# Block results stored from ScalarE's queue, the last round's weights in half-width transfers, and three steps of the dense part in another order

## The chip, the cores and the metric

One core of a Trainium2 chip runs the whole program. The metric is the device time of one execution in microseconds (us); the median of three timed runs stands for the kernel. A profile is one further execution, recorded instruction by instruction.

## The reference, cut to what matters

One sequence of 256 tokens with 1,024 features goes through two layers, all in float32. Layer 0 has a mixer (one input projection, attention of 8 heads beside a gated convolution, an output projection) and a SwiGLU of width 2,816. Layer 1 has a state-space mixer, whose tables are computed from parameters, and a top-2-of-8 expert SwiGLU of width 3,584. Each sub-layer is normed, scaled and shifted by values made from a condition vector `c`, and added back through a gate:

```python
h = _ada_norm(x, norm_mix_g[layer], sh_m, sc_m)
...
probs = jax.nn.softmax(logits, axis=-1)
top_p, top_i = lax.top_k(probs, TOP_K)
...
for e in range(N_EXPERTS):
    out = out + gates[:, e:e + 1] * _swiglu(hf, w_gate[e], w_up[e], w_down[e])
```

## The kernel before

Each engine has its own instruction stream; semaphores join them. SyncE (SP) only issues DMAs. Weights come from DRAM in one order through a ring of buffers.

**Dense part.** A piece of weights is 128 rows of 8 KB (1 MB); the ring has 14 places, and SP loads piece n once TensorE has counted `piece_done` to n - 13. TensorE first multiplies the condition by pieces of `mod_w` (L483), then does the input projection, 12 pieces (L499). Ahead of that, VectorE scales the normed input in eight chunks (L1173), and ScalarE adds the shift to each chunk (`shift(0)`, L925): only then is the input of the projection there. In ScalarE's stream `shift(0)` (L941) stands behind five DMA issues: one that loads the small state-space parameters (L937) and four that fill a scratch tensor (L939). Behind it stand the exponential and the sines (L943 to L946), for which VectorE waits at L1223.

**Layer 0's SwiGLU.** `FF_UNITS` = 11 units. For unit f TensorE does gate (one piece), up (one piece), and down of unit f - 1 (one piece); behind each of the three is a slot numbered 3f, 3f+1, 3f+2 in which steps of the state-space tables may stand (`segment`, L638). `side_plan` (L89) gives each of four batches q its four steps s: slots 5+7q+s, so the batches start in slots 5, 12, 19 and 26. Step 0 transposes `bsm`, which VectorE makes in `block_inputs(q)` (L1368, six operations over 128x1024) behind its product of unit 1, 3, 5 or 8 (L1393, the condition at L1397); TensorE waits for it at L611. ScalarE takes each step's result out of PSUM (L989) and sends whole tables to a scratch tensor: `bt_spilled` behind step 1, `ct_spilled` behind step 2, `kc_spilled` behind step 3 (L993 to L1010). SP loads them back when all four batches have been sent. VectorE also computes part of the `mod` values in the same units (`mod_dots`, L1198), each waiting for a 1 MB piece that ScalarE's stream issues (L1016).

**Experts.** Tokens are gathered into blocks of 32, here 22 blocks. The expert width is cut into 7 rounds of 512. In a round each expert has three pairs of pieces (2 MB each: two for gate and up, one for down), and each of its blocks does `gate_up` (L795, 64 matmuls in the trace), ScalarE's Silu (L1088), VectorE's product and transpose, and `e_down` (L804, 32). `gate_up` of block j+1 stands ahead of `e_down` of block j on TensorE. Nine places hold pairs, so a pair is loaded when the third expert before it is through (`pair_plan`, L131; the loads at L415). 168 pairs in all, 24 in a round.

**Last round.** VectorE adds the round's result to a block, multiplies by the gate row (`scale_block`, L1582) and counts `y_scaled`. The blocks of experts 0 to 6 but the last one, here 19, go to the scratch tensor `y_scr`, from which GpSimd fetches each token's two rows by index (L1771) when all have landed (L1765); the last three blocks go through a matmul instead (L832). A store of a block (L431) is one DMA of 128 KB: 32 rows of `y_scr`, seen as 4 quarters x 32 rows x 256 numbers, so 128 pieces of 1 KB. SP's stream issues the stores: those of expert 0 behind the load of pair 158, expert 1's behind 161, expert 2's behind 164 (`STORED_EARLY` = 3), and the rest behind the last load, 167. Behind them is one more load, the final gain (L451). The fetched rows overwrite the place of pair 159.

Of the kernel before, what the change touches and what calls it, by code (L numbers as in the profile page):

```python
# [22 lines left out]
T = 256  # L23
# [63 lines left out]


def side_plan():  # L89

    uses = {("param", 0): 2, ("param", 1): 2, ("param", 2): 1, ("param", 3): 1}
    at = {}
    for q in range(BATCHES):
        for s in range(4):
            at.setdefault(5 + 7 * q + s, []).append(("param", q, s))
    plan, use = {}, 0
    for n in sorted(at):
        for kind, i, s in at[n]:  # L100
            plan.setdefault(n, []).append((kind, i, s, use))
            use += uses[kind, s]
    return plan
# [46 lines left out]
LAST_E = EXPERTS - 1  # L150
FILLS = -(-MOST * BLK // T)
STORED_EARLY = 3
STORE_FROM = PAIRS - STORED_EARLY * STEP
FREE_AT = Y_PAIR // STEP % EXPERTS
# [18 lines left out]
def trunk_kernel(nc, xt_in, pos_in, cols_in, gain_in, consts_in, ssm_in, c_in, rows_in, dense_in, expert_in, ssm_scr, kc_scr, y_scr, out):  # L173
    ctx = ExitStack()
    with ctx:
# [170 lines left out]
        def pair_slot(n):  # L346
            s = PAIR_PLAN[n][0]
            if s < RING // 2:
                return ring[:, 2 * s * PIECE:(2 * s + 2) * PIECE]
            s = MORE - 1 - (s - RING // 2)  # L350
            return more[:, 2 * s * PIECE:(2 * s + 2) * PIECE]

        def pair_sem(n):
            s = PAIR_PLAN[n][0]
            return ring_full[2 * s] if s < RING // 2 else (more_full0, more_full1)[s - RING // 2]

        def pair_full(n):

            s = PAIR_PLAN[n][0]
            dense_uses = sum(parts(m) for m in range(PRE) if m % RING == 2 * s) if s < RING // 2 else 0  # L360
            return pair_sem(n), 16 * (dense_uses + sum(PAIR_PLAN[m][0] == s for m in range(n + 1)))

# [22 lines left out]
        def _(sp):  # L385
# [28 lines left out]
            def load_pair(n):  # L414
                sp.dma_start(pair_slot(n), expert_in[n]).then_inc(pair_sem(n), 16)  # L415

# [4 lines left out]
            for n in range(RING // 2, RING // 2 + SOON):  # L421
                sp.wait_ge(piece_done, AT_GLU)
                load_pair(n)

            def store_rows(upto, e):

                if e == 0:
                    sp.wait_ge(y_stored, 16 * FILLS)
                with sp.Fori(upto[e - 1] if e else 0, upto[e] if e < LAST_E - 1 else upto[e] - 1) as j:
                    sp.wait_ge(y_scaled, j + 2)  # L430
                    sp.dma_start(y_scr[bass.ds(j * BLK, BLK), :].rearrange("i (q n) -> q i n", q=4),  # L431
                                 acc[:, bass.ds(j * 256, 256)]).then_inc(y_stored, 16)

            sp.wait_ge(items_ready, 1)
            upto = blocks_upto(sp)
            for n in range(RING // 2 + SOON, PAIRS):
                prior = PAIR_PLAN[n][1]
                if prior is None:
                    sp.wait_ge(e_gather, GATHERS)
                else:  # L440
                    step, k = divmod(prior, STEP)
                    rnd, e = divmod(step, EXPERTS)
                    sp.wait_ge(gu_done if k < GU else down_done, upto[e] + upto[-1] * rnd)
                load_pair(n)
                if STORE_FROM - 1 <= n < PAIRS - 1 and n % STEP == GU:
                    store_rows(upto, (n + 1 - STORE_FROM) // STEP)

            for e in range(STORED_EARLY, LAST_E):
                store_rows(upto, e)
            sp.wait_ge(gu_done, upto[FREE_AT] + upto[-1] * (ROUNDS - 1))  # L450
# [444 lines left out]
        def _(act):  # L895
# [38 lines left out]
            act.wait_ge(piece_done, AT["mod", 5] + 1)  # L934
            act.dma_start(posi, pos_in.partition_broadcast(P).rearrange("p o t -> p (o t)")).then_inc(pos_loaded, 16)
            act.wait_ge(piece_done, AT["mod", 7] + 1)
            act.dma_start(ssm_par[:, :], ssm_in).then_inc(ssm_loaded, 16)  # L937
            for q in range(BATCHES):
                act.dma_start(kc_scr[q, P:P + GCH * (LB - 1), :].rearrange("a b -> (a b)").rearrange("(p n m) -> p n m", p=P, n=2),  # L939
                              consts_in[:, C_ID + P:C_ID + P + GCH * (LB - 1)].unsqueeze(1).broadcast_to([P, 2, GCH * (LB - 1)])).then_inc(kc_zeroed, 16)  # L940
            shift(0)  # L941
            act.wait_ge(decay_arg, 1)
# [144 lines left out]
            def silu():  # L1087
                return act.activation(e_act_b, PS[:, 0, 0:SLOT], ACT.Silu)  # L1088
# [5 lines left out]
            for e in range(EXPERTS):  # L1094
# [10 lines left out]
                with act.Fori(upto[e - 1] + 1 if e else 1, upto[e]) as j:  # L1105
                    act.wait_ge(gu_done, j + 1)
                    silu().then_inc(silu_ready, 1)
            for rnd in range(1, ROUNDS):
                with act.Fori(0, upto[-1]) as j:
                    act.wait_ge(gu_done, j + upto[-1] * rnd + 1)  # L1110
                    silu().then_inc(silu_ready, 1)
            act.activation(held, consts[:, C_EPS:C_EPS + 1], ACT.Sqrt)
            for t_ in range(2):
# [13 lines left out]
        def _(dve):  # L1127
# [260 lines left out]
            for f in range(FF_UNITS):  # L1388
# [7 lines left out]
                for q in range(1, BATCHES):  # L1396
                    if (5 + 7 * (q - 1) + 2) // 3 + 1 == f:  # L1397
                        block_inputs(q)
# [228 lines left out]
            dve.nop().then_inc(gt_ready, 1)  # L1627
            dve.nop().then_inc(y_scaled, 1)
            with dve.Fori(1, upto_6) as j:
# [46 lines left out]
        def _(pool):  # L1676
# [84 lines left out]
            for rnd in range(1, ROUNDS):  # L1761
                with pool.Fori(0, upto[-1]) as j:
                    pool.wait_ge(gu_done, j + upto[-1] * rnd)
                    load_block(j).then_inc(hbuf_ready, 1)
            pool.wait_ge(y_stored, upto[LAST_E - 1] * 16 + 16 * (FILLS - 1))  # L1765
            pool.sem_inc(y_all, 1)
# [113 lines left out]
```

## Time and profile before

| | us |
|---|---|
| median of 3 runs | 1461.38 (1456.54 to 1463.14) |
| the profiled execution | 1464.03 |
| its span, first to last instruction | 1462.2 |
| TensorE busy | 1370.1 (94%) |
| VectorE busy | 405.6 |
| ScalarE busy | 150.9 |
| GpSimd busy | 169.1 |

The span is 1.8 us shorter than the profiled execution's own time. TensorE's mean granted clock in it was 0.98. Read a timeline row as start, length, engine, line, operation, output <- inputs, count, and in brackets the idle time of that engine just before, with what ended it. PE is TensorE, DVE VectorE, ACT ScalarE, POOL GpSimd, SP SyncE; a q behind the name means its instruction queue, as in a DMA issue. "PEld" is TensorE's weight load.

### The profile page before, as it was taken

To read this page: it belongs to the slowest core of one execution; us is meant where nothing else is said; L and a number is where in the kernel's file an instruction comes from. 1 tells how busy PE (TensorE), PEld (TensorE's weight loads), DVE (VectorE), ACT (ScalarE), POOL (GpSimd) and SP (SyncE) were. 2 spreads that over 40 slices of the span, in tenths; PEclk is the share of its full clock that TensorE was granted. 3 is DMA by queue.
4 is the path that set the end of the run, shared out by engine and by line. 5 is a ranking of instruction groups with operands and counts; after the bars stand their busy time and mean duration, and the time that the engine had idled before them with its cause. 6 is when DMAs were issued, how large, how long until landed. Compare 5 with 4: busy or idle time off the path is not lost.

```text
span 1462.2 us, 43274 instructions
## 1 busy us (share of the span) xinstructions
PE 1370.1 (94%) x19076; PEld 1046.7 (72%) x19076; DVE 405.6 (28%) x1018; ACT 150.9 (10%) x362; POOL 169.1 (12%) x244
## 2 busy tenths in 40 slices
PE   4999999999998898999999989989989999999984
PEld 3887788888787786766677767757757776766762
DVE  2825251453515616111111111111111111111224
ACT  2202121000003104100000000000000000000001
POOL 0000052351401300000000000000000000000001
PEclk8999999999999999999999999999999999999997
DMA  9947578777467507779999999999999999999984
GB/s 383 422 184 302 232 270 282 273 298 284 171 236 288 203 1 308 326 282 427 426 421 414 427 425 414 427 426 408 427 426 411 418 426 424 417 425 426 407 343 170
DMA packets 52818, 499.93 MB, mean 342 GB/s; under 512 B 6668, under 2 KB 13964, under 8 KB 15372
## 3 DMA queue, kind: packets, MB, share of 16 engines
q1 hardware_dynamic: 45708, 463.36, 77.3%
q10 hardware_dynamic: 6400, 32.39, 5.9%
q8 instruction: 120, 1.97, 0.5%
q0 software_dynamic: 576, 2.10, 0.4%
q14 instruction: 14, 0.11, 0.0%
HBM read 485.38 MB, written 16.58 MB: 343 GB/s over the span
## 4 chain that ended last, share of the span: by engine, by line
PE 74%; DMA 15%; DVE 4%; SPq 3%; issue 1%; ACT 1%; POOL 0%; ACTq 0%; POOLq 0%; DVEq 0%
PE PS L795 29%; PE PS L499 19%; PE PS L804 14%; DMA ring<-in_expert_stream 9%; PE PS L649 4%; SPq L431 2%; DMA arena<-in_mod_rows 2%; DVE arena L1137 2%; DMA arena<-in_expert_stream 2%; DMA ring<-in_dense_stream 2%; PE PS L775 2%; PE PS L483 1%; PE PS L531 1%; PE PS L473 1%; PE PS L703 1%
## 5 line engine op out<-in xcount | busy, mean ns | idle before, releaser
L795 PE MATMUL PS<-ring,arena 128*32 128x256 f32 x8288 | 483.2, 381 | 26.1 <-DMA ring<-in_expert_stream 21.7
L795 PEld LDWEIGHTS PS<-ring,arena 128*32 128x32 f32 x8288 | 313.5, 110 | 164.7 <-DMA ring<-in_expert_stream 19.1
L499 PE MATMUL PS<-arena,ring 128*128 128x256 f32 x1408 | 311.9, 383 | 6.2 <-ACT arena L925 4.6
L499 PEld LDWEIGHTS PS<-arena,ring 128*128 128x128 f32 x1408 | 268.7, 192 | 46.0 <-issue 7.1
L804 PE MATMUL PS<-ring,arena 128*32 128x256 f32 x3456 | 208.6, 379 | 0.0
L1137 DVE TENSOR_TENSOR stat<-stat,PS 128x128 f32<-128x128 f32 x154 | 44.4, 288 | 515.4 <-ACT stat L1088 515.4
L804 PEld LDWEIGHTS PS<-ring,arena 128*32 128x32 f32 x3456 | 130.3, 110 | 56.8 <-issue 0.6
L1750 POOL COPY arena<-arena 128x256 f32 x153 | 61.5, 402 | 791.7 <-PE PS L795 791.7
L1137 DVE TENSOR_TENSOR arena<-arena,PS 128x256 f32 (+1 forms) x142 | 63.3, 446 | 238.6 <-PE PS L804 161.6
L1088 ACT ACTIVATE stat<-PS 128x128 f32<-128x128 f32 x154 | 43.2, 280 | 782.4 <-PE PS L795 782.4
L795 PE MATMUL PS<-arena 128*32 128x256 f32 x1568 | 94.8, 379 | 4.3 <-DMA ring<-in_expert_stream 4.3
L804 PE MATMUL PS<-arena 128*32 128x256 f32 x1472 | 89.0, 379 | 0.8 <-DVE consts L1137 0.8
L795 PEld LDWEIGHTS PS<-arena 128*32 128x32 f32 x1568 | 60.0, 110 | 29.3 <-issue 5.7
L649 PE MATMUL PS<-arena,ring 128*128 128x256 f32 x352 | 78.4, 382 | 0.0
L649 PEld LDWEIGHTS PS<-arena,ring 128*128 128x128 f32 x352 | 67.0, 192 | 9.4 <-DVE arena L1137 0.4
L804 PEld LDWEIGHTS PS<-arena 128*32 128x32 f32 x1472 | 56.8, 110 | 23.6 <-issue 1.1
L1137 DVE TENSOR_TENSOR arena<-arena 128x32 f32<-128x32 f32 (+9 forms) x146 | 64.7, 467 | 12.7 <-ACT arena L899 6.5
L899 ACT ACTIVATE arena<-PS 128x512 f32<-128x512 f32 (+4 forms) x72 | 39.2, 560 | 249.4 <-PE PS L499 63.4
L1203 DVE SCALAR_TENSOR_TENSOR arena<-arena 128x1024 f32<-128x1024 f32 x28 | 41.2, 1509 | 78.2 <-DMA arena<-in_mod_rows 78.2
L483 PE MATMUL PS<-ring,arena 128*32 128x128 f32 x1088 | 35.2, 286 | 15.1 <-DMA consts<-in_consts 10.7
L1567 DVE STREAM_TRANSPOSE arena<-stat 128x128 f32<-128x128 f32 x154 | 46.8, 304 | 2.3 <-PE PS L804 2.3
L483 PEld LDWEIGHTS PS<-ring,arena 128*32 128x32 f32 x1088 | 30.5, 115 | 19.9 <-DMA consts<-in_consts 10.7
(206 smaller groups left out, 624.6 us busy)
## 6 DMA issues: line engine op xcount, KB each, us to landing
ring<-in_expert_stream SPq DMA_DIRECT2D x133, 2048.0 KB, 21.7
ring<-in_dense_stream SPq DMA_DIRECT2D x91, 1024.0 KB, 9.3
arena<-in_expert_stream SPq DMA_DIRECT2D x35, 2048.0 KB, 20.1
arena<-in_mod_rows ACTq DMA_DIRECT2D x14, 1024.0 KB, 6.5
ssm_scratch<-arena ACTq DMA_DIRECT2D x8, 1024.0 KB, 10.0
ring<-ssm_scratch SPq DMA_DIRECT2D x8, 1024.0 KB, 8.7
ring<-kc_scratch SPq DMA_DIRECT2D x32, 128.0 KB, 2.4
y_scratch<-arena SPq DMA_DIRECT2D x19, 128.0 KB
```

Source lines behind the costliest of these rows:

```text
L431: sp.dma_start(y_scr[bass.ds(j * BLK, BLK), :].rearrange("i (q n) -> q i n", q=4), acc[:, bass.ds(j * 256, 256)]).then_inc(y_stored, 16)
L483: mm = pe.matmul(to[32 * q:32 * q + 32], cond[:, 32 * (4 * h + c):32 * (4 * h + c) + 32], w[:, c, q, :], start=(h == 0 and c == 0), stop=( ...
L499: mm = pe.matmul(PS[:, bank, j * T:(j + 1) * T], w[:, c, j * P:(j + 1) * P], moving[:, c, :], start=(c == 0), stop=(c == NC - 1))
L649: mm = pe.matmul(PS[:, 4 + n // 2, (n % 2) * T:(n % 2 + 1) * T], w[:, j * D + n * P:j * D + (n + 1) * P], f_hid[:, (f % 2) * 512 + j * T:( ...
L795: mm = pe.matmul(PS[32 * q:32 * q + 32, 0, 0:256], hbuf[:, c * BLK:(c + 1) * BLK], w[:, q * 256:(q + 1) * 256], start=(c == 0), stop=(c == ...
L804: mm = pe.matmul(PS[32 * q:32 * q + 32, 1, 0:256], hidT[:, ch * BLK:(ch + 1) * BLK], w[:, q * 256:(q + 1) * 256], start=(ch == 0), stop=(c ...
L899: return act.activation(out_ap, in_ap, ACT.Copy)
L1088: return act.activation(e_act_b, PS[:, 0, 0:SLOT], ACT.Silu)
L1137: return dve.tensor_tensor(o_, a, b, op)
L1203: d = dve.scalar_tensor_tensor(mod_piece[:, i * D:(i + 1) * D], mod_piece[:, i * D:(i + 1) * D], 1.0, cond_row, ALU.mult, ALU.mult, accum_ ...
L1567: return dve.transpose(hidT, e_hid_b)
L1750: return pool.tensor_copy(hbuf, hg[:, bass.ds(j * 256, 256)])
```

## The change

The 19 stores leave SP's stream and stand in ScalarE's, in its loop over the last round's blocks: behind the Silu of block j it waits for `y_scaled` and issues the store of block j - 2 (`BEHIND` = 2). Each pair of the last round (n from 144, `HALVED`) is loaded by two DMAs of 128 rows of 8 KB in place of one with rows of 16 KB; TensorE still waits for both halves. In the dense part `shift(0)` stands ahead of the five DMA issues, and the tables' batches 2 and 3 start in slots 20 and 28 in place of 19 and 26.

```diff
+PARAM_AT = (5, 12, 20, 28)
...
-            at.setdefault(5 + 7 * q + s, []).append(("param", q, s))
+            at.setdefault(PARAM_AT[q] + s, []).append(("param", q, s))
...
-STORED_EARLY = 3
-STORE_FROM = PAIRS - STORED_EARLY * STEP
+BEHIND, FILLS = 2, -(-MOST * BLK // T)
+HALVED = PAIRS - EXPERTS * STEP
...
@@ pair_full
-            return pair_sem(n), 16 * (dense_uses + sum(PAIR_PLAN[m][0] == s for m in range(n + 1)))
+            return pair_sem(n), 16 * (dense_uses + sum(1 + (m >= HALVED) for m in range(n + 1) if PAIR_PLAN[m][0] == s))
@@ SyncE
             def load_pair(n):
-                sp.dma_start(pair_slot(n), expert_in[n]).then_inc(pair_sem(n), 16)
+                if n < HALVED:
+                    sp.dma_start(pair_slot(n), expert_in[n]).then_inc(pair_sem(n), 16)
+                    return
+                for at in (slice(0, PIECE), slice(PIECE, 2 * PIECE)):
+                    sp.dma_start(pair_slot(n)[:, at], expert_in[n][:, at]).then_inc(pair_sem(n), 16)
...
-            def store_rows(upto, e):
-
-                if e == 0:
-                    sp.wait_ge(y_stored, 16 * FILLS)
-                with sp.Fori(upto[e - 1] if e else 0, upto[e] if e < LAST_E - 1 else upto[e] - 1) as j:
-                    sp.wait_ge(y_scaled, j + 2)
-                    sp.dma_start(y_scr[bass.ds(j * BLK, BLK), :].rearrange("i (q n) -> q i n", q=4),
-                                 acc[:, bass.ds(j * 256, 256)]).then_inc(y_stored, 16)
...
-                if STORE_FROM - 1 <= n < PAIRS - 1 and n % STEP == GU:
-                    store_rows(upto, (n + 1 - STORE_FROM) // STEP)
-
-            for e in range(STORED_EARLY, LAST_E):
-                store_rows(upto, e)
@@ ScalarE
+            shift(0)
             act.wait_ge(piece_done, AT["mod", 7] + 1)
             act.dma_start(ssm_par[:, :], ssm_in).then_inc(ssm_loaded, 16)
             for q in range(BATCHES):
                 act.dma_start(kc_scr[q, ...
-            shift(0)
...
-            for rnd in range(1, ROUNDS):
+            for rnd in range(1, ROUNDS - 1):
                 with act.Fori(0, upto[-1]) as j:
                     act.wait_ge(gu_done, j + upto[-1] * rnd + 1)
                     silu().then_inc(silu_ready, 1)
+            rnd = ROUNDS - 1
+            act.wait_ge(y_stored, 16 * FILLS)
+            with act.Fori(0, BEHIND) as j:
+                act.wait_ge(gu_done, j + upto[-1] * rnd + 1)
+                silu().then_inc(silu_ready, 1)
+            with act.Fori(BEHIND, upto[-1] - 1) as j:
+                act.wait_ge(gu_done, j + upto[-1] * rnd + 1)
+                silu().then_inc(silu_ready, 1)
+                act.wait_ge(y_scaled, j)
+                act.dma_start(y_scr[bass.ds(j * BLK - BEHIND * BLK, BLK), :].rearrange("i (q n) -> q i n", q=4),
+                              acc[:, bass.ds(j * 256 - BEHIND * 256, 256)]).then_inc(y_stored, 16)
+            act.wait_ge(gu_done, upto[-1] * ROUNDS)
+            silu().then_inc(silu_ready, 1)
@@ VectorE
-                    if (5 + 7 * (q - 1) + 2) // 3 + 1 == f:
+                    if (PARAM_AT[q - 1] + 2) // 3 + 1 == f:
                         block_inputs(q)
...
-            dve.nop().then_inc(y_scaled, 1)
+            dve.nop().then_inc(y_scaled, BEHIND - 1)
@@ GpSimd
-            pool.wait_ge(y_stored, upto[LAST_E - 1] * 16 + 16 * (FILLS - 1))
+            pool.wait_ge(y_stored, upto[-1] * 16 + 16 * (FILLS - BEHIND - 1))
```

`block_inputs(3)` stays in unit 8 (both forms of the condition give it), `block_inputs(2)` in unit 5. With 22 blocks the stores are the same 19, and both counts of GpSimd's wait ask for all of them.

## Rows read from the trace of the kernel before

**Rows 1.** The page: rates of DMA in 40 slices; shares of the chain that ended last.
```profile
GB/s 383 422 184 302 232 270 282 273 298 284 171 236 288 203 1 308 326 282 427 426 421 414 427 425 414 427 426 408 427 426 411 418 426 424 417 425 426 407 343 170
PE 74%; DMA 15%; DVE 4%; SPq 3%; issue 1%; ACT 1%; POOL 0%; ACTq 0%; POOLq 0%; DVEq 0%
```
**Rows 2.** The chain in order of time, 24 to 46: start, length, what.
```profile
30.30 0.35 ACTq L937
...
34.20 0.52 ACT arena L925
...
34.85 11.24 PE PS L499 x42
```
**Rows 3.** Timeline, 20 to 110: the scaling, and VectorE's first operation behind the sines.
```profile
31.76 3.25 DVE L1173 SCALAR_TENSOR_TENSOR buf_b<-arena,acol,stat 128x256 f32<-128x256 f32 x8
...
41.16 0.46 DVE L1137 TENSOR_TENSOR arena<-arena 128x288 f32<-128x288 f32 x1 [3.04 <-ACT arena L946]
...
80.22 0.69 DVE L1137 TENSOR_TENSOR arena<-PS,arena 128x512 f32<-128x512 f32 x1 [5.68 <-PE PS L517]
```
**Rows 4.** Timeline, 305 to 450, TensorE: the two late steps 0 and what follows each.
```profile
305.92 7.07 PE L649 MATMUL PS<-arena,ring 128*128 128x256 f32 x32
...
329.37 1.97 PE L616 MATMUL PS<-consts,arena 128*128 128x128 f32 x8 [2.57 <-DVE arena L1137]
...
331.13 7.66 PE L649 MATMUL PS<-arena,ring 128*128 128x256 f32 x32
...
385.84 1.09 PE L616 MATMUL PS<-consts,arena 128*128 128x128 f32 x8 [3.30 <-DVE arena L1137]
...
386.77 8.76 PE L499 MATMUL PS<-arena,ring 128*128 128x256 f32 x32
```
**Rows 5.** Windows: length, busy time of each engine, granted clock, DMA share, GB/s.
```profile
329.00:332.30 3.30, 2.93 (x11) 2.75 (x12) 3.21 (x6) 0.21 (x1) 0.00 (x0) 0.50 0.56 233
...
387.00:390.30 3.30, 3.30 (x9) 2.64 (x8) 1.08 (x2) 0.68 (x2) 0.00 (x0) 0.50 0.00 0
```
**Rows 6.** Timeline, 360 to 450: VectorE behind unit 9, the last table sent.
```profile
403.35 0.69 DVE L1137 TENSOR_TENSOR arena<-arena,PS 128x512 f32<-128x512 f32 x1 [15.27 <-PE PS L499]
...
412.10 0.33 ACTq L1010 DMA_DIRECT2D kc_scratch<-arena  x1
```
**Rows 7.** Timeline, 1285 to 1438, SyncE's stores; the last row is line 431 alone.
```profile
1363.39 2.12 SPq L431 DMA_DIRECT2D y_scratch<-arena  x2
...
1378.92 13.31 SPq L431 DMA_DIRECT2D y_scratch<-arena  x6
...
1395.22 15.24 SPq L431 DMA_DIRECT2D y_scratch<-arena  x3
...
1413.52 23.41 SPq L431 DMA_DIRECT2D y_scratch<-arena  x8
...
L431 SPq DMA_DIRECT2D y_scratch<-arena x19: 585/668/13882, 1363.4 to 1436.3; - x19
```
**Rows 8.** A window with stores alone in flight; line 939's transfers, issue to landing.
```profile
1432.70:1438.00 5.30, 5.08 (x96) 3.63 (x96) 1.30 (x4) 1.35 (x2) 0.00 (x0) 1.00 0.29 100
...
DMA to landing us min/median/max: 14.4/21.1/27.9
```
**Rows 9.** Timeline, 1385 to 1462: a block's Silu, TensorE's stalls, and the end.
```profile
1397.10 0.28 ACT L1088 ACTIVATE stat<-PS 128x128 f32<-128x128 f32 x1 [4.90 <-PE PS L795]
...
1408.58 1.93 PE L795 MATMUL PS<-ring,arena 128*32 128x256 f32 x32 [2.87 <-DMA ring<-in_expert_stream]
...
1432.92 3.66 PE L795 MATMUL PS<-ring,arena 128*32 128x256 f32 x64 [1.59 <-DMA arena<-in_expert_stream]
...
1444.56 1.17 POOL L1771 DMA_INDIRECT arena<-y_scratch,slots_i  x1 [14.36 <-POOLq L1766]
...
1445.53 2.09 PE L832 MATMUL PS<-consts 32*128 32x256 f32 x16 [2.37 <-DVE consts L1137]
...
1449.15 1.28 DVE L1660 SCALAR_TENSOR_TENSOR arena<-arena,PS 128x1024 f32<-128x1024 f32 x1 [3.67 <-DMA arena<-y_scratch,slots_i]
```

More of the change, by code:

```diff
@@ L150 @@
 LAST_E = EXPERTS - 1
-FILLS = -(-MOST * BLK // T)
-STORED_EARLY = 3
-STORE_FROM = PAIRS - STORED_EARLY * STEP
+BEHIND, FILLS = 2, -(-MOST * BLK // T)
+HALVED = PAIRS - EXPERTS * STEP
+assert FILLS > BEHIND + 1
 FREE_AT = Y_PAIR // STEP % EXPERTS
```

## The prediction
> **What bounds the kernel now.** I read the page first. Its rates [rows 1] fall into two parts: up to slice 18 DMA moves 170 to 330 GB/s with room to spare, from slice 19 it stands at 407 to 428. The chain's shares [rows 1] are 74% TensorE and 15% DMA. So up to some 590 us TensorE bounds, and a stall taken from it is a gain that stays, because the experts' loads start when its dense pieces are done. In the experts DMA bounds, and there only the end can be changed by where the stores stand. I then read the chain in order of time through the dense part [rows 2], the timeline where TensorE waits for an engine [rows 3, 4], the clock there [rows 5], and last SyncE's queue and the tail [rows 7 to 9].
>
> **shift(0) ahead of the issues.** ScalarE begins an issue at 30.30 and five of them hold it until 34.15; its first shifted chunk starts at 34.20 and TensorE at 34.85 [rows 2]. VectorE's eight scaled chunks take 3.25 us from 31.76, 0.41 each [rows 3], so the first is there at 32.2 and the shift can start then: 34.20 - 32.2 = 2.0 us. Both engines go chunk by chunk at 0.41, so the 2.0 hold for the whole projection. What is now late: the five issues (3.85 us) fall behind the shift, which ends at about 35.3, then the sines. They started behind 34.20 + 3.30 = 37.5 and now behind 35.3 + 3.85 = 39.2, so VectorE's operation at 41.16 [rows 3] comes 1.7 us later. VectorE's chain runs into the rotations; there it waits 5.68 us for TensorE before the second one [rows 3], and that covers 2.0 + 1.7 = 3.7. Value 2.0, bounds 0 (TensorE's clock stays low longer) and 2.7.
>
> **The batches' steps.** Step 0 of batch 2 stalls TensorE for 2.57 us, step 0 of batch 3 for 3.30, both waiting for VectorE [rows 4]. Behind each, the granted clock is 0.50 for one stretch [rows 5]: of the two levels the lower, 1.2 GHz, after TensorE had stood idle for 2.57 and 3.30 us. The price shows beside rows at the full clock: L649 x32 takes 7.66 us against 7.07, the step's eight transposes 1.97 against 1.09 (itself partly slow), L499 x32 8.76 against 7.07 [rows 4]. That is 0.59 + 0.88 = 1.5 for the first and 1.7 for the second. Together 2.57 + 3.30 + 1.5 + 1.7 = 9.1 us.
>
> Does the new order cover them? Batch 2 moves behind down(5), 7.07 us of TensorE work: bsm was 2.57 late, so 4.5 us of cover are left. Batch 3 moves two slots, behind gate(9) and up(9), 14 us: 3.30 late, and TensorE comes 4.1 us earlier by the first repair; 14 - 3.3 - 4.1 = 6.6 left. The other steps move with them: the copy and the scratch transfer of step 1 of batch 2 now fall in unit 7, ahead of its `mod` pieces, one megabyte in the same queue. VectorE's product of a unit waited 15.27 us for TensorE in unit 9 [rows 6], so lateness of a few us there is hidden. The last table to be sent was issued at 412.10 [rows 6]; it now stands two slots later, but behind a TensorE that is 11 us ahead, so at about 417, and what needs it (the projection of the state-space part) comes some 30 us later. Value 8.7 (a little kept back for a unit that now waits for its `mod` pieces), bounds 5 and 9.2. Dense part: -10.7.
>
> **The stores.** First what a store costs. In the window where stores alone are in flight the DMA share is 0.29 of 16 engines, 4.6, at 100 GB/s [rows 8]: a store of 131 KB runs on four engines (the odd 0.6 is other traffic) and holds them 1.31 us, although several were waiting. So all stores go to the same four engines, 19 x 1.31 = 25 us of their time, while a pair's load (2.1 MB at 427 GB/s [rows 1]) holds all sixteen for 4.9. A load has landed when the slowest engine is through, so the four decide.
>
> Second, how two queues share an engine. Line 939's four transfers are 1,024 pieces of 448 bytes, issued on ScalarE's queue at 30.68 to 34.15 while SyncE's 8 KB rows were queued. They landed 14.4 to 27.9 us after issue [rows 8], the first at 45.1, the last at 61.4: 48 pieces per engine in 16.3 us, 0.34 each. A row of 8 KB takes 0.31 at full rate. One small piece goes through per row of the other queue. A store has 32 pieces on each of its engines: beside 8 KB rows it lasts 32 x (0.31 + 0.04) = 11.3 us, beside 16 KB rows it would last 21. That is what the halved loads change; the loads' own bytes and rate stay, and 24 more issues of 0.4 us on SyncE are hidden.
>
> A block takes 5.18 us (a Silu of 0.28 behind a wait of 4.90 [rows 9]), so stores are issued twice as fast as they are served while loads are queued. From about 1332 to 1429 some 8.5 are served; before, 2 + 6 + 3 = 11 stood ahead of the last pair [rows 7]. The last pair is then (11 - 8.5) x 1.31 = 3.3 us earlier; TensorE's last wait for DMA ends at 1432.9 [rows 9], now at 1429.6, and its last scatter ends at 1444.3 instead of 1447.6. But the four engines' total is the same, and they were never idle for long: what is not served before the last pair is served behind it, 10.5 x 1.31 = 13.8 us, until 1443.4, and the gain row's load (512 KB, 1.2 us) shares that time where it stood behind the stores. GpSimd started at 1444.56 [rows 9] and starts at 1444.5 to 1445.7. VectorE's final sum already waits for the fetched rows (3.67 us, until 1449.15 [rows 9]), not for TensorE. So the gain of 3.3 on TensorE is not on the path: the end moves by 0 to +1.2. Value +1.0, bounds -9 and +20, the mechanisms of rivals C and A below.
>
> **Sum.** 1464.03 - 2.0 - 8.7 + 1.0 = 1454.3 for the profiled execution. Its own time stands 2.65 above the median 1461.38, so the median becomes 1461.4 - 9.7 = **1451.7**.
>
> **Rivals.**
> *A. ScalarE is held in its own issue.* SyncE's 19 issues take 0.67 us in the middle, but one took 13.9 [rows 7], and the groups of 6, 3 and 8 stores took 13.3, 15.2 and 23.4 us, though at 1.25 a piece they would take 7.5, 3.8 and 10: a queue takes only so many pieces. Here some nine stores pile up, where SyncE had three to five. Held ScalarE is a late Silu, behind it VectorE's product and all of TensorE. Against it: the long issues came only with loads ahead in the same queue, and between them SyncE got five stores off in a row. Price: SyncE's three groups were held 5.8, 11.4 and 13.4 us beyond their 1.25 a piece; less the 4.3 that a block hides each time (its 4.90 of wait less an issue), 18 us of delay for TensorE, whose last scatter then ends at 1462. From the final sum's start to the end of the span it is 13.05 us (1449.15 to 1462.2), so the end comes at 1475, +13, and the whole at 1461.4 - 10.7 + 13 = 1464. If four blocks in a row run at a store's 11.3 in place of 5.18, the delay is 25 us, the end at +20, the whole 1471. It decides from a delay of 15 us: with more, the end loses over 10.7 and the kernel is slower than before.
> *B. Stores pass in bunches.* If ScalarE's queue is served ahead, 17 stores stand before the last pair, 6 more than before: 6 x 1.31 = 7.9 later, TensorE ends at 1455.5, and 13.05 behind it the end stands at +6.4: whole 1457.1. The even passing of pieces [rows 8] speaks against it.
> The Trainium skill, "DMA: Bandwidth & Descriptors", section on queues, rings and completion order, says that an engine drains a whole packet of several descriptors from one ring before it switches; by that a store would pass in a few turns, which is this rival. The trace's pieces went one by one.
> *C. The stores leave the four engines' way.* If ScalarE's queue used other engines, or they had room, TensorE loses its four stalls (the first 2.87, the last 1.59 [rows 9], 7.6 in all), the fetch starts early, and 13.05 behind 1440.0 stands the end: -9, whole 1441.6. The Trainium skill, same page, on how many engines a transfer uses, says a HWDGE transfer takes the lowest-numbered ones whatever the queue; no row here shows that for ScalarE's queue, and by it this rival falls.
> *D. The dense gain is half* (a `mod` piece late for a unit's product): -5 +1: 1457.4.
>
> **How the numbers follow.** Forecast 0.45; A 0.30 (0.20 near 1464, 0.10 near 1471); B 0.10; C 0.07; D 0.08. No change that a measurement can tell is 0.5%, 7.3 us: 1454.1 to 1468.7. Faster: most of the forecast (0.43) and C: 0.50. Slower: the far end of A: 0.09. The rest, 0.41, within. Range: A's near case belongs in it, C and A's far case not: 1446 to 1467. The forecast's own range is 1447 to 1456.
>
> **What would show it.** Right: TensorE's first L499 at about 32.9; no wait of L616 for VectorE and no half clock around 330 and 387; VectorE's L1411 near 428.5 instead of 439.3; all SyncE issues of the last round short; the last pair near 1419 (1429.6 less 10.7), but GpSimd's L1771 still at about 1434, and L1660 waiting for it. Wrong: issues of ScalarE over 5 us and gaps between Silus of 11 us; TensorE's last-round waits named ScalarE or VectorE; a new wait for L616 or of L499 for VectorE's product in units 7 to 9.

## The result, and the profile after

The changed kernel is **slower**: 1469.59 us median (1466.71 to 1473.09) against 1461.38 (1456.54 to 1463.14), with five timed runs behind each median. The ratio is 1.0061, 95% interval 1.0040 to 1.0081. Forecast were 1451.7 and a range of 1446 to 1467. The mechanism is that of rival A (ScalarE held in its own issue). The time stands beside its far case (1471), but the account below shows that the stores' price was nearer its near case, and that the dense part's gain was missing. The profiled execution took 1468.12, with a span of 1466.3; before, 1464.03 and 1462.2.

The page after, rates of DMA in 40 slices and shares of the chain (before: [rows 1]):
```profile
GB/s 385 422 179 309 227 278 277 277 299 306 122 278 350 108 4 417 211 392 426 426 405 427 425 426 420 425 422 415 426 427 409 426 427 410 424 419 422 358 332 101
PE 79%; DMA 12%; ACTq 3%; DVE 3%; issue 1%; ACT 1%; POOL 0%; SPq 0%; another core or an unknown queue 0%; DVEq 0%; POOLq 0%
```
The DMA-bound stretch begins one slice earlier (392 in slice 18, where 282 stood), so the dense part is shorter. And the chain has ACTq with 3%, 44 us, where [rows 1] had 0%: that says where to look.

The dense part, timeline (start, length, engine, line, what, idle before it and its releaser); these rows answer [rows 2 to 4]:
```profile
32.57 3.26 DVE L1180 SCALAR_TENSOR_TENSOR buf_b<-arena,acol,stat 128x256 f32<-128x256 f32 x8
...
33.74 30.46 PE L493 MATMUL PS<-arena,ring 128*128 128x256 f32 x128 [2.69 <-ACT arena L919]
...
42.60 0.46 DVE L1144 TENSOR_TENSOR arena<-arena 128x288 f32<-128x288 f32 x1 [3.67 <-ACT arena L940]
...
326.19 7.07 PE L643 MATMUL PS<-arena,ring 128*128 128x256 f32 x32
333.10 1.04 PE L610 MATMUL PS<-consts,arena 128*128 128x128 f32 x8
...
391.53 1.04 PE L610 MATMUL PS<-consts,arena 128*128 128x128 f32 x8
...
431.40 5.41 PE L467 MATMUL PS<-arena,consts 128*128 128x256 f32 x16 [2.00 <-ACT arena L906]
449.23 17.42 PE L697 MATMUL PS<-arena,ring 128*128 128x128 f32 x128 [0.88 <-DVE arena L1435]
...
576.70 0.28 ACT L1082 ACTIVATE stat<-PS 128x128 f32<-128x128 f32 x1 [3.22 <-PE PS L789]
```
The same two places in the kernel before:
```profile
441.27 5.41 PE L473 MATMUL PS<-arena,consts 128*128 128x256 f32 x16 [2.00 <-ACT arena L912]
...
584.35 0.28 ACT L1088 ACTIVATE stat<-PS 128x128 f32<-128x128 f32 x1 [3.23 <-PE PS L795]
```
TensorE starts 1.17 us behind the start of the scaling, before 3.09 ([rows 2, 3]). Both steps 0 (L610, the two rows without brackets) carry no wait, and the 32 matmuls ahead of the first take 7.07, as do those behind it. TensorE reaches the modulation sums (L467) 9.9 us earlier. L697, 16.11 us before, takes 17.42 here. The first Silu of the experts is 7.6 us earlier. Up to here the profiled execution does what was forecast (10.7), less 3 us.

The last round, ScalarE alone (its Silus on L1082, its stores on L1115):
```profile
1347.82 6.04 ACTq L1115 DMA_DIRECT2D y_scratch<-arena  x1
1354.28 0.28 ACT L1082 ACTIVATE stat<-PS 128x128 f32<-128x128 f32 x1 [6.42 <-issue]
1354.54 9.42 ACTq L1115 DMA_DIRECT2D y_scratch<-arena  x1
1364.38 0.28 ACT L1082 ACTIVATE stat<-PS 128x128 f32<-128x128 f32 x1 [9.82 <-issue]
1364.64 3.64 ACTq L1115 DMA_DIRECT2D y_scratch<-arena  x1
1371.32 0.28 ACT L1082 ACTIVATE stat<-PS 128x128 f32<-128x128 f32 x1 [6.67 <-PE PS L789]
...
1392.29 0.58 ACTq L1115 DMA_DIRECT2D y_scratch<-arena  x1
...
1397.47 9.45 ACTq L1115 DMA_DIRECT2D y_scratch<-arena  x1
1407.33 0.28 ACT L1082 ACTIVATE stat<-PS 128x128 f32<-128x128 f32 x1 [9.83 <-issue]
1407.59 9.57 ACTq L1115 DMA_DIRECT2D y_scratch<-arena  x1
1417.59 0.28 ACT L1082 ACTIVATE stat<-PS 128x128 f32<-128x128 f32 x1 [9.98 <-issue]
1417.84 6.75 ACTq L1115 DMA_DIRECT2D y_scratch<-arena  x1
1425.01 0.28 ACT L1082 ACTIVATE stat<-PS 128x128 f32<-128x128 f32 x1 [7.15 <-issue]
```
The five stores ahead of 1347.82 go off in 0.6 us each (the first in 1.2), then three are held; after the pause five go off again, then three are held. "[9.82 <-issue]" in front of a Silu reads: ScalarE was idle for 9.82 us and nothing that the profile knows of as work released it; the row above tells what it stood in. The six held issues take 44.87 us. What they cost is read at the Silu behind each: it stands behind an idle time of 6.42, 9.82, 6.67, 9.83, 9.98 and 7.15 us, where an undisturbed block has 4.90 [rows 9], so the six come 20.5 us late in all. TensorE's waits named for VectorE and issue make up 13.3 of them; in the windows below its granted clock falls to 0.67 and 0.89. Its waits from 1310 to 1442, those of the kernel before in the same window (L795; one of 0.8 left out), and three windows (length, busy time of PE, PEld, DVE, ACT, POOL, granted clock, DMA share, GB/s):
```profile
PE PS L789 <- DVE stat L1144: 9.3, 4, 4.7
PE PS L789 <- issue: 4.0, 1, 4.0
PE PS L789 <- DMA ring<-in_expert_stream: 2.7, 1, 2.7
```
```profile
PE PS L795 <- DMA ring<-in_expert_stream: 10.0, 5, 2.9
PE PS L795 <- DMA arena<-in_expert_stream: 1.6, 1, 1.6
```
```profile
1360.00:1370.00 10.00, 5.29 (x56) 2.67 (x52) 1.15 (x4) 0.28 (x1) 0.00 (x0) 0.67 0.69 286
...
1400.00:1410.00 10.00, 6.03 (x96) 3.39 (x92) 1.18 (x5) 0.28 (x1) 0.40 (x1) 0.89 1.01 421
...
1430.00:1440.00 10.00, 10.00 (x193) 7.26 (x187) 3.61 (x11) 0.45 (x2) 1.15 (x3) 1.00 0.15 48
```
VectorE's product, itself behind the Silu, releases TensorE. While it is held the loads catch up: its waits for weights fall from 11.6 us to 2.7, and 20.5 less these 8.9 is about what the round loses below. In 1360 to 1370 even the weights' stream falls to 286 GB/s, since TensorE frees no buffer; that is how a held ScalarE costs a kernel that DMA bounds. Of the stores left behind the last pair, forecast at 13.8 us, some 8 are there: by the landings in the trace (a transfer's signals that it is through) the pair is in at 1425.8, forecast near 1419, and the next six stores end by 1433.7. ScalarE had already paid for the rest.

The tail, and the last Silu, where [rows 9] had the last scatter (L832) at 1445.53:
```profile
1439.83 0.28 ACT L1082 ACTIVATE stat<-PS 128x128 f32<-128x128 f32 x1 [4.90 <-PE PS L789]
...
1444.24 0.31 DVE L1574 STREAM_TRANSPOSE arena<-stat 128x128 f32<-128x128 f32 x1 [3.81 <-remote]
...
1452.57 2.09 PE L826 MATMUL PS<-consts 32*128 32x256 f32 x16 [2.37 <-DVE consts L1144]
...
1454.72 1.28 DVE L1667 SCALAR_TENSOR_TENSOR arena<-arena,PS 128x1024 f32<-128x1024 f32 x1 [2.21 <-PE PS L826]
```
The last round takes 134.6 us from its first Silu (1305.2) to its last, before 123.4 (1313.3 to 1436.6): +11.2, more than the dense part had gained. GpSimd fetches the rows from 1439.27, early, and VectorE's final sum now waits for TensorE, no longer for the rows. One more pause, 3.81 us of VectorE at 1440.4, has a releaser that the profile can't name. Four of the fourteen traces have such a one near this place, of 3.4 to 3.8 us, the other three in kernels at 1449 to 1450; the edits don't tell those four from the rest, and its cause stays open.

### The profile page after: what moved, and what is told of

It is laid out like the page before. It is cut to its first block, busy times and chain, and to the rows that moved or that the text cites. A ratio compares the mean times of both kernels' runs of the same rounds, so it can differ in the third digit from the quotient of the medians.

```text
span 1466.3 us, 43233 instructions
## 1 busy us (share of the span) xinstructions
PE 1374.6 (94%) x19076; PEld 1065.5 (73%) x19076; DVE 404.5 (28%) x1018; ACT 150.9 (10%) x362; POOL 170.9 (12%) x244
## 4 chain that ended last, share of the span: by engine, by line
PE 79%; DMA 12%; ACTq 3%; DVE 3%; issue 1%; ACT 1%; POOL 0%; SPq 0%; another core or an unknown queue 0%; DVEq 0%; POOLq 0%
PE PS L789 30%; PE PS L493 21%; PE PS L798 14%; DMA ring<-in_expert_stream 9%; PE PS L643 5%; ACTq L1115 3%; PE PS L769 2%; DMA arena<-in_expert_stream 2%; DMA ring<-in_dense_stream 2%; PE PS L477 1%; PE PS L525 1%; PE PS L467 1%; PE PS L697 1%; DVE arena L1144 1%; PE PS L610 0%
## 5 line engine op out<-in xcount | busy, mean ns | idle before, releaser
L789 PE MATMUL PS<-ring,arena 128*32 128x256 f32 x8288 | 490.9, 383 | 27.6 <-DMA ring<-in_expert_stream 16.8
L789 PEld LDWEIGHTS PS<-ring,arena 128*32 128x32 f32 x8288 | 326.7, 111 | 157.4 <-issue 26.6
L798 PE MATMUL PS<-ring,arena 128*32 128x256 f32 x3456 | 213.3, 380 | 0.0
L798 PEld LDWEIGHTS PS<-ring,arena 128*32 128x32 f32 x3456 | 136.1, 110 | 52.7 <-issue 1.5
L1082 ACT ACTIVATE stat<-PS 128x128 f32<-128x128 f32 x154 | 43.1, 280 | 793.3 <-PE PS L789 750.1
L789 PE MATMUL PS<-arena 128*32 128x256 f32 x1568 | 97.7, 384 | 7.6 <-DVE stat L1144 5.3
L798 PE MATMUL PS<-arena 128*32 128x256 f32 x1472 | 91.6, 384 | 3.2 <-DVE consts L1144 3.2
L789 PEld LDWEIGHTS PS<-arena 128*32 128x32 f32 x1568 | 61.8, 111 | 32.7 <-issue 11.0
L798 PEld LDWEIGHTS PS<-arena 128*32 128x32 f32 x1472 | 59.0, 111 | 25.6 <-issue 5.2
L477 PE MATMUL PS<-ring,arena 128*32 128x128 f32 x1088 | 35.7, 287 | 16.5 <-DMA consts<-in_consts 10.7
L477 PEld LDWEIGHTS PS<-ring,arena 128*32 128x32 f32 x1088 | 30.6, 115 | 21.7 <-DMA consts<-in_consts 10.7
```

The costliest lines, as they stand in the source:

```text
L477: mm = pe.matmul(to[32 * q:32 * q + 32], cond[:, 32 * (4 * h + c):32 * (4 * h + c) + 32], w[:, c, q, :], start=(h == 0 and c == 0), stop=( ...
L789: mm = pe.matmul(PS[32 * q:32 * q + 32, 0, 0:256], hbuf[:, c * BLK:(c + 1) * BLK], w[:, q * 256:(q + 1) * 256], start=(c == 0), stop=(c == ...
L798: mm = pe.matmul(PS[32 * q:32 * q + 32, 1, 0:256], hidT[:, ch * BLK:(ch + 1) * BLK], w[:, q * 256:(q + 1) * 256], start=(ch == 0), stop=(c ...
```

## The experiments

Each is compared with the kernel before, run beside it on the same chip. "Last round" is the time from its first Silu to its last.

**1. One half alone.** The dense part's two edits in the kernel before:
```diff
+PARAM_AT = (5, 12, 20, 28)
...
-            at.setdefault(5 + 7 * q + s, []).append(("param", q, s))
+            at.setdefault(PARAM_AT[q] + s, []).append(("param", q, s))
...
+            shift(0)
             act.wait_ge(piece_done, AT["mod", 7] + 1)
...
-            shift(0)
```


> The kernel before with the dense part's two edits alone (shift(0) ahead of the issues, batches 2 and 3 in slots 20 and 28); the stores stay in SyncE's stream. Theory (the dense edits give 9.9 us, the stores' move takes more than that back): 1451 to 1453 against 1461.4, TensorE's first matmul of layer 1 some 9.9 us earlier and the last round as before, 136 us from its first Silu to the end. Rival (the experts' part does not keep the dense gain, because DMA bounds it): 1459 to 1462, with the 9.9 us seen up to 560 us and gone by the last round.

Measured 1456.03, ratio 0.9968 (0.9956 to 0.9981), before 1460.23: 4.2 us of the 10.7 that the prediction gave the dense part, and between the two answers. Its profile has the first Silu at 576.3, as early as in the changed kernel, and yet that execution is the slowest of eleven (1457.94).

The changed kernel with those two edits undone:
```diff
-PARAM_AT = (5, 12, 20, 28)
+PARAM_AT = (5, 12, 19, 26)
...
-            shift(0)
             act.wait_ge(piece_done, AT["mod", 7] + 1)
...
+            shift(0)
```


> The changed kernel with the dense edits undone: only the stores in ScalarE's stream and the halved loads. Theory: 1469.6 + 9.9 = 1478 to 1481, the same six long issues of ScalarE (6 to 10 us each, 35 to 45 in sum). Rival (the loss comes from both parts meeting, as the loads now start at another moment): 1462 to 1470.

Measured 1467.99, ratio 1.0054 (1.0035 to 1.0073): the stores alone cost 0.54%, 7.9 us. It falls in the rival's range, though not for the rival's reason: the stores cost about the same with and without the dense edits (last round 133.7 and 134.6 us), and ScalarE has its long issues here too (five, of 6.7 to 9.6 us). My own number had added the forecast gain of the dense part back to 1469.6, and the changed kernel is not faster than this one. So the dense gain, not the stores' price, was what I had too large here.

**2. How long a store lasts.** The weight pairs of the last round in one transfer (16 KB rows), and in four (4 KB rows):
```diff
-                for at in (slice(0, PIECE), slice(PIECE, 2 * PIECE)):
+                for at in [slice(c * 2 * PIECE // 1, (c + 1) * 2 * PIECE // 1) for c in range(1)]:
...
+                for at in [slice(c * 2 * PIECE // 4, (c + 1) * 2 * PIECE // 4) for c in range(4)]:
```
The first new line is that of the whole pairs, the second that of the quarters; the count of landings that TensorE waits for goes with each.


> The changed kernel with the last round's pairs loaded whole, rows of 16 KB. Theory (one 1 KB piece passes per row of the other queue, so a store lasts 32 x 0.65 = 21 us beside 16 KB rows instead of 11.3, and ScalarE is held longer): 5 to 15 us slower than the changed kernel, 1475 to 1485, long issues of ScalarE of 15 to 20 us. Rival (the halved loads fill SyncE's own queue and are what costs): faster than the changed kernel, 1455 to 1465, and ScalarE's issues short.

Measured 1478.32, ratio 1.0130 (1.0108 to 1.0151), as the theory had it; two issues are held, for 16.6 and 22.6 us.

> The changed kernel with the last round's weight pairs in four transfers of 4 KB rows in place of two of 8 KB. Theory (the four engines that carry a store give it one piece between two rows of the weights, so the length of a row sets how long a store lasts, and that alone sets when ScalarE's queue is full): an 8 KB row takes about 0.31 us of an engine and a store 11.3 us; a 4 KB row takes half, a store some 32 x (0.155 + 0.04) = 6.2 us, little over the 5.2 us in which TensorE makes a block, so ScalarE is held in its own issues not at all or for under 5 us in all (the changed kernel: about 45 us), and the time is 1453 to 1462. Rival (the number of transfers outstanding in ScalarE's queue sets it, or the stores only share four engines whose bytes are too many): the holds stay, 1466 to 1472. A third outcome: SyncE, whose queue was already full with halves (2.0 to 3.2 us an issue), falls behind with twice the issues and TensorE waits for weights: over 1472, with SyncE's issues long and no hold in ScalarE's.

Measured 1466.06, ratio 1.0032 (1.0014 to 1.0049). The stores' issues on line 1115, shortest, median and longest in ns: whole pairs, then quarters; and what TensorE waited for in 1340 to 1430, whole pairs:
```profile
L1115 ACTq DMA_DIRECT2D y_scratch<-arena x19: 584/585/22622, 1323.2 to 1450.3; - x19
...
PE PS L789 <- issue: 17.1, 1, 17.1
PE PS L789 <- DVE stat L1144: 11.1, 1, 11.1
```
```profile
L1115 ACTq DMA_DIRECT2D y_scratch<-arena x19: 585/585/1205, 1322.9 to 1431.9; - x19
...
PE PS L789 <- DMA ring<-in_expert_stream: 9.1, 4, 3.4
...
1400.00:1410.00 10.00, 7.61 (x112) 4.12 (x104) 1.24 (x4) 0.28 (x1) 0.40 (x1) 0.83 0.97 343
```
With quarters no issue is held at all: same queue, same stores, only the loads are cut finer. From the landings of the stores: beside 4 KB rows one ends every 5.9 us (forecast 6.2), beside 8 KB rows every 10.3 (forecast 11.3; ends at 1336.0, 1346.3, 1356.5, 1366.9), beside 16 KB rows every 15 to 24 (forecast 21), and in the pause of loads after 1370 one every 1.35 (forecast 1.31). The Trainium skill, "DMA: Bandwidth & Descriptors", Queues, rings and completion order, has an engine drain a packet of typically 9 to 17 descriptors before it turns to the next ring. The rates here don't agree: 10.3 us for 32 pieces is 0.32 us a piece, about the 0.31 of one 8 KB row.

But of the changed kernel's 0.61% over before only half went, and the theory's 1453 to 1462 was missed; the third outcome's sign (SyncE's issues long, TensorE waiting for weights) came with the rival's time. It isn't SyncE that is late, though. The stores now get through while loads are queued, so their bytes stand in front of the pairs on four engines. A quartered pair gives 64 landings; of the one that TensorE waits for until 1410.66, 48 were in by 1398.1, and the last 16, a quarter of them, came from 1404.4 to 1410.6. The same is seen in the kernel before: of the pair behind its longest stall, until 1408.58 [rows 9], twelve of 16 landings were in by 1406.9 and four came at 1408.4 to 1408.5. So the hold was one of two prices of a four-engine store, and the kernel before already paid the other.

**3. Sixteen engines for a store.** Each store as four transfers of 32 rows, one for each group of partitions, so that each is split over all engines:
```diff
-                act.dma_start(y_scr[bass.ds(j * BLK - BEHIND * BLK, BLK), :].rearrange("i (q n) -> q i n", q=4),
-                              acc[:, bass.ds(j * 256 - BEHIND * 256, 256)]).then_inc(y_stored, 16)
+                for q in range(4):
+                    act.dma_start(y_scr[bass.ds(j * BLK - BEHIND * BLK, BLK), q * 256:(q + 1) * 256],
+                                  acc[BLK * q:BLK * (q + 1), bass.ds(j * 256 - BEHIND * 256, 256)]).then_inc(y_stored, 16)
```
The count that GpSimd waits for goes with it.


> The changed kernel with each block stored by four DMAs of 32 rows of 1 KB (one for each quarter) in place of one DMA of 4 x 32 x 1 KB. Same bytes, same pieces, same queue, four issues in place of one. Theory (a store uses as many engines as its outermost count allows: 4 before, 16 now): 8 pieces per engine and store in place of 32, 2.8 us beside the loads, no pile, no long issue of ScalarE, no engine 25 us behind the others; the last pair lands some 7 us earlier than with the stores on SyncE: 1443 to 1450. Rival (ScalarE is held by the count of pieces or of DMAs in its queue, wherever they run): 1465 to 1480, long issues as before or more of them.

Measured **1448.86**, ratio 0.9925 (0.9906 to 0.9944), in the theory's range; the longest issue is 1.0 us.

The same with whole pairs in the last round:

> The run with ScalarE's stores spread over 16 engines (1448.9), with the weight pairs of the last round whole again (16 KB rows). Theory (one piece between two rows): a store's 8 pieces on each engine then last 8 x (0.61 + 0.04) = 5.2 us, just the time of a block, so holds of ScalarE appear only in bunches; 1449 to 1455, and far under the 1478.3 of whole pairs with four-engine stores. Rival (the number of DMAs outstanding in ScalarE's queue, now four a block, is what fills it): long issues as with whole pairs before, 1465 to 1480.

Measured **1447.35**, ratio 0.9907 (0.9887 to 0.9927), the lowest median of all and under the theory's 1449 to 1455. Its issues, and TensorE's waits in 1340 to 1430 with the window that stood at clock 0.67 in the changed kernel:
```profile
L1116 ACTq DMA_DIRECT2D y_scratch<-arena x76: 327/328/1162, 1322.2 to 1419.5; - x76
...
PE PS L798 <- DVE consts L1145: 0.8, 1, 0.8
PE PS L789 <- DMA ring<-in_expert_stream: 0.6, 1, 0.6
...
1360.00:1370.00 10.00, 10.00 (x192) 7.27 (x187) 2.47 (x8) 0.47 (x2) 0.80 (x2) 1.00 1.01 414
```
No hold, hardly a wait for weights, full clock; the last round takes 115.4 us (118.3 with halved pairs, 123.4 before, 134.6 after). Four times the issues cost ScalarE nothing: 4 x 0.33 us beside a wait of 4.9. My time for a store beside whole pairs was off (5.2 us; the landings show up to 7.3, and up to 24.5 us from a store's first issue to its last landing). So these stores too were served more slowly than the 5.18 us of a block, and up to four were outstanding. On sixteen engines a store puts 8 pieces in each ring where it put 32 in four, and the round was over before the queue was full. Halving the pairs helped the stores that sit on four engines (1478.32 to 1469.59); beside the spread ones it brought nothing that the intervals tell (1448.86 against 1447.35).

The spread stores in SyncE's queue, in the kernel with the dense edits:
```diff
-                    sp.dma_start(y_scr[bass.ds(j * BLK, BLK), :].rearrange("i (q n) -> q i n", q=4),
-                                 acc[:, bass.ds(j * 256, 256)]).then_inc(y_stored, 16)
+                    for q in range(4):
+                        sp.dma_start(y_scr[bass.ds(j * BLK, BLK), q * 256:(q + 1) * 256],
+                                     acc[BLK * q:BLK * (q + 1), bass.ds(j * 256, 256)]).then_inc(y_stored, 16)
```


> The kernel before with the two edits of the dense part, its stores left in SyncE's queue, but each store issued as four transfers of 32 rows, so that it has the 16 engines to itself in turn instead of four. Theory (what hurts or helps is how many engines carry a store, not which engine's queue issues it): about the time of the run with ScalarE's stores spread (1448.9), 1446 to 1452; the stores then take 2 to 4 us each behind one pair in the queue. Rival (the queue itself matters: SyncE's stores wait behind 16 KB rows that were queued ahead and hold back the next pairs): 1453 to 1458, no better than the run with the dense edits alone (1456.0).

Measured 1452.42, ratio 0.9947 (0.9928 to 0.9966), between the two answers. By the medians, beside the run with the dense edits alone (1456.03), the spread is worth 3.6 us in SyncE's queue, and ScalarE's queue another 3.6 to 5.1 (1448.86, 1447.35); of these steps only the one to 1447.35 is clear of overlapping intervals, and barely. In SyncE's queue TensorE still waits for weights:
```profile
PE PS L799 <- DMA ring<-in_expert_stream: 6.3, 3, 2.9
```

**4. The dense part's 4 us for 10.** Each edit alone, beside the old stores:

> The kernel before with the later places of two batches' steps alone; first shift and stores as before. The two dense edits together gave 4.2 us in the medians (1460.2 to 1456.0) and 8.0 us at the first expert block in the profile. Theory (the gain of the dense part is TensorE's and the batches' steps carry most of it): first Silu of the experts 5.5 to 7 us earlier than before, time 1455.5 to 1458. Rival (the first shift carries most): under 2 us earlier at the first Silu and a time within 0.5 us of before.

> The kernel before with the earlier first shift alone; batches' steps and stores as before. Both dense edits gave 4.2 us in the medians (1460.2 to 1456.0), the batches' steps alone 1.3 us with an interval that holds no change. Theory A (the profile's sizes hold: first shift 2 us, steps 8.7 us, and what a profile shows at the first expert block is given back by the DMA-bound rounds in equal share): the shift alone is worth 0.5 to 1 us, 1459.5 to 1460.5. Theory B (the parts are worth what the medians say, and the shift carries the rest, 3 us or more): 1456.5 to 1458.

Measured 1459.64, ratio 0.9997 (0.9985 to 1.0008), and 1459.60, ratio 1.0000 (0.9983 to 1.0017): neither differs from before. For the shift that is theory A. The steps alone had the theory's sign in the trace (first Silu at 576.0, 8.4 us earlier) without its time. And beside spread stores with whole pairs: the shift alone, the steps alone, neither.

> The best version so far (ScalarE's stores spread over 16 engines, weight pairs whole, 1447.35) without the later places of the batches' steps; the earlier first shift stays. In it the last round has no hold and hardly a wait, so the dense part's gain should come through undiluted. Theory A (steps 8.7 us at the first expert block, 6 to 8 us at the end): 1453 to 1456. Theory B (the steps are worth 1 to 2 us at the end, since the weights' stream, which the DMA engines bound, doesn't start earlier for it): 1448 to 1450.

> The best version so far (1447.35) with the batches' steps later and the first shift at its old place. Theory A (shift 2 us at most): 1448 to 1449.5. Theory B (the shift carries 3 us or more in the medians): 1450 to 1452.

> The kernel before with ScalarE's stores spread over 16 engines alone: no dense edit, weight pairs whole. Theory A (both dense edits together worth 8 us once the last round lets them through): 1455 to 1457. Theory B (they are worth the 4 us that the medians showed beside the old stores): 1450 to 1452.5. The stores' own part is then before less this: 4 to 6 us by A, 8 to 11 us by B.

Measured 1450.17 (ratio 0.9931, 0.9913 to 0.9948), 1448.86 (0.9915, 0.9896 to 0.9933) and 1449.62 (0.9927, 0.9910 to 0.9944); with both edits it was 1447.35 (0.9907). That is theory B's small steps and theory A's small shift; with neither edit the time is just under theory B's 1450. So both together are worth 0.2% there, 2.3 us of medians, with intervals that overlap, and the stores, spread and in ScalarE's queue, 10.6 us without them. The trace of the kernel with neither edit says why the forecast was too large. TensorE at the two late steps (the code of the dense part is that of the kernel before):
```profile
328.86 1.09 PE L610 MATMUL PS<-consts,arena 128*128 128x128 f32 x8 [1.54 <-DVE arena L1145]
329.79 7.07 PE L643 MATMUL PS<-arena,ring 128*128 128x256 f32 x32
...
382.43 1.09 PE L610 MATMUL PS<-consts,arena 128*128 128x128 f32 x8 [1.83 <-DVE arena L1145]
383.36 7.07 PE L493 MATMUL PS<-arena,ring 128*128 128x256 f32 x32
...
578.82 0.28 ACT L1082 ACTIVATE stat<-PS 128x128 f32<-128x128 f32 x1 [3.19 <-PE PS L789]
```
The same waits as in [rows 4], but of 1.54 and 1.83 us in place of 2.57 and 3.30, and behind them 7.07 at once, no half clock (granted 1.00 in 329 to 332.3). In the third trace of that dense code, the run with the stores alone, they are 2.08 and 1.93 (granted 0.69). The first Silu is at 578.8, with no edit made. Over all traces: without the dense edits it is at 584.3, 582.6 and 578.8 (mean 581.9), with both at 575.0 to 577.4 (seven, mean 576.5), with one of them at 576.0 to 577.9 (four). So either edit alone shows at that place what both show together: their gains don't add up there. By the start of the last round the seven stand at 1304.4 to 1308.4 and the three at 1308.2 to 1313.7: 5.4 us between the means at both places, of which the medians show 2 to 4. The times of one kernel spread over 4 to 14 us; what the medians lack of the 5.4 isn't settled.

## Why the prediction was wrong

**The stores: this step failed.** It said: with what is left behind the last pair "the end moves by 0 to +1.2", value +1.0. The stores alone measured +7.9 (5.1 to 10.7). The working had the right rate: a store on four engines, one piece to a row, 11.3 us (measured 10.3), against a block of 5.18. From there it let some nine stores pile up in ScalarE's queue at no cost, a queue depth for which it gave no row, and had the price of the contrary as rival A. The pile can't form: with about three stores in flight the issue is held. At the first hold (1347.82) five had been issued and two had landed, and it ended at 1353.86, three quarters through the third. [Rows 7] had the sign of it, 13.3, 15.2 and 23.4 us for groups of 6, 3 and 8 stores; I put them down to the loads in that queue. The rate that I had worked out was itself the argument for A: issued every 5.2 us and served every 10.3, the stores would be some nine deep by the end of the round, and the only question was whether the queue is that deep.

**Rival A was the right mechanism**: its signs (issues over 5 us, gaps of 9.8 us between Silus, TensorE's waits named for VectorE and issue) are all there. In size it was the near case: a delay of 20.5 us at the Silus (18 in the near case, 25 in the far) and +11.2 for the last round, +7.9 in the medians of the stores alone (+13 and +20). That the time came out by the far case's 1471 and not by the near one's 1464 is luck: both had taken off a dense gain of 10.7 that beside these stores no median shows. The forecast's sign of short issues on SyncE failed as well, up to 5.6 us for a half pair, but no wait for weights over 2.7 us followed.

**shift(0):** forecast -2.0. TensorE starts 1.17 us behind the scaling against 3.09 in the profile, 1.9. That TensorE's time is gained there was right; alone it moves no median.

**The batches' steps: the largest term, -8.7, was mis-sized.** Both waits went and the half clock with them, as forecast. But the 9.1 us were a size of one execution: in another of the same dense code they are 3.4 us and no half clock. Alone the steps moved no median (ratio 0.9997). Part of what is left comes back as a slower L697 (17.42 for 16.11). At the first Silu the whole dense part is worth 5.4 us on the mean of the traces, for 10.7. In medians it is worth 4.2 beside the old stores, 2.3 beside the spread ones and nothing beside the four-engine stores in ScalarE's queue (1469.59 with it, 1467.99 without).

**Rival D** (dense gain half, 1457.4) thus happened too, by another cause than the one I named. **B** and **C** fell: the stores end evenly, every 10.3 us, and not in a bunch, and those of ScalarE's queue sit on four engines that the loads use too. The Trainium skill, "DMA: Bandwidth & Descriptors", Why a DMA increments its semaphore by 16 and not by 1, has a HWDGE transfer of this kind (one that SyncE or ScalarE issues) on the lowest-numbered engines; the trace agrees as far as it goes, four landings a store and four late ones a pair, but it doesn't number the engines. Spreading the stores made by hand what C had hoped for: 10.6 us for the spread and the move together, where C had 9.

**The sum again:** stores +8 and dense -2 to -4 would be +4 to +6; measured were +8.2 (5.8 to 11.8), which is the stores alone. Why the dense edits give 4.2 us in one kernel and none in another stays open.

## What to carry to other kernels

Before a transfer is moved to an engine with other work, divide its service time (pieces on its busiest DMA engine, times the time of the other queue's row) by its issue interval. Above one the transfers pile up; if the pile outgrows the queue before the stretch is over, the issuing engine stands still, and everything behind it. At 10.3 us for 5.2 it did; at 5.9, and at up to 7.3 with a quarter of the pieces in each ring, the 19 stores were over first. Cure the shape first: a store whose outer dimension is 4 sat on four engines, and moving it to ScalarE's queue added 0.5%; the same move with four transfers of 32 rows took 0.7% off. A stall of 2 or 3 us and a half clock read in one execution are a sample: look for the same place in a second trace of the same code before its whole length goes into the sum.

## What the runs showed of the hardware

- A queue held its issuing engine with about three four-engine stores in flight (5 issued, 2 landed and 0.75 of the next: 1353.86), for up to 9.57 us beside 8 KB rows and 22.62 beside 16 KB rows. With 8 pieces in each of sixteen rings none of 76 issues took over 1.16 us, though up to four stores were outstanding.
- The length of the rows of *another* queue sets the time of a small-piece transfer: a store every 5.9, 10.3 and some 15 to 24 us beside rows of 4, 8 and 16 KB, every 1.35 with no load in flight (four engines each time).
- Four engines that carry stores are late for the loads as well: of a quartered pair's 64 landings the last 16 came 6.3 to 12.5 us behind the 48th, and of the whole pair behind the longest stall of the kernel before the last four of 16 came 1.5 us behind the twelfth.
- Each four-engine store leaves five landings, one about 1 us behind the issue and four when its engines are through. The Trainium skill, "DMA: Bandwidth & Descriptors", Why a DMA increments its semaphore by 16 and not by 1, has the issuing sequencer write the rest of the increment at once; the five (95 for 19 stores) agree.
- Quarters of a pair cost SyncE: its 50 issues in 1340 to 1425 took 328 to 4344 ns, medians 1.34 us for the ring's and 0.54 for the arena's.
